# The delta-rule layer of a hybrid decoder on one core: query products behind the joins, the two decay exponentials apart

## The reference, cut to what matters

```python
decay = jnp.exp(jnp.where(causal, gc[..., :, None] - gc[..., None, :], -jnp.inf))
kb = k * beta[..., None]
a = jnp.where(strict, jnp.einsum('bhnid,bhnjd->bhnij', kb, k) * decay, 0.0)
sol = lax.linalg.triangular_solve(a + eye, rhs, left_side=True, lower=True)
u, w = sol[..., :dv], sol[..., dv:]
qk = jnp.where(causal, jnp.einsum('bhnid,bhnjd->bhnij', q, k) * decay, 0.0)
q_dec = q * jnp.exp(gc)[..., None]
def step(state, inp):
    v_new = u_c - jnp.einsum('bhcd,bhde->bhce', w_c, state)
    o = jnp.einsum('bhcd,bhde->bhce', qd_c, state) + jnp.einsum('bhij,bhje->bhie', qk_c, v_new)
    state = state * cd_c[..., None, None] + jnp.einsum('bhcd,bhce->bhde', kd_c, v_new)
    return state, o
```

## Time and profile before

| | |
|---|---|
| median of 3 runs | 3050.88 us (3050.23 to 3052.8) |
| profiled execution, its time | 3050.12 us |
| its span, first to last instruction | 3048.4 us |
| TensorE busy | 2762.6 us (91%) |
| VectorE, ScalarE, GpSimd busy | 1563.2, 866.6, 779.0 us |
| mean granted TensorE clock | 0.95 of full speed |
| delta-rule layer | about 40 to 820 us of the span |
| one head of its loop | 91.7 us |

### The profile page before, as it was taken

One profiled execution on the slowest core, in us unless ns is written; L12 is line 12 of the kernel. 1 busy time (PEld: TensorE's weight loads), 2 busy tenths in 40 slices (PEclk: granted clock), 3 DMA queues, 4 the chain that ended last, 5 costly groups with the idle time before them and its releaser, 6 DMA issues. The chain is left out here.

```text
span 3048.4 us, 35919 instructions
## 1 busy us (share of the span) xinstructions
PE 2762.6 (91%) x13277; PEld 2296.6 (75%) x13277; DVE 1563.2 (51%) x1780; ACT 866.6 (28%) x1213; POOL 779.0 (26%) x372
## 2 busy tenths in 40 slices
PE   7789898888597999999998599999688999999996
PEld 5677777777576888888887487788576888888885
DVE  4455545555234454544455675567354454444555
ACT  5244444344332111111111334333332111111112
POOL 2333223332142222222222211111232222222223
PEclk8799999999798999999999799999898999999998
DMA  2010110010242111111111310110332111111112
GB/s 106 21 42 28 34 41 34 28 41 7 71 151 83 49 48 48 48 41 55 48 48 48 119 35 31 46 48 34 130 119 77 49 41 48 55 48 48 48 62 97
DMA packets 62892, 172.11 MB, mean 56 GB/s; under 512 B 6177, under 2 KB 23137, under 8 KB 62833
## 3 DMA queue, kind: packets, MB, share of 16 engines
q1 hardware_dynamic: 62832, 171.33, 16.5%
HBM read 146.11 MB, written 25.20 MB: 56 GB/s over the span
## 5 line engine op out<-in xcount | busy, mean ns | idle before, releaser
L151 POOL TENSOR_TENSOR f_wlo<-f_raw,f_whi 128x1024 fp32r<-128x1024 f32 x132 | 335.6, 2551 | 1082.8 <-ACT f_whi L171 1082.8
L61 PE MATMUL f_up<-x_hi,f_whi 128*128 128x512 f32 x1408 | 550.4, 391 | 23.0 <-POOL f_wlo L151 23.0
L62 PE MATMUL f_up<-x_lo,f_whi 128*128 128x512 f32 x1408 | 549.7, 390 | 0.0
L63 PE MATMUL f_up<-x_hi,f_wlo 128*128 128x512 f32 x1408 | 549.6, 390 | 0.0
L171 ACT ACTIVATE f_whi<-f_raw 128x1024 fp32r<-128x1024 f32 x132 | 139.8, 1059 | 935.5 <-PE f_up L63 505.9
L61 PEld LDWEIGHTS f_up<-x_hi,f_whi 128*128 128x128 f32 x1408 | 265.6, 189 | 79.1 <-POOL f_wlo L151 23.8
L62 PEld LDWEIGHTS f_up<-x_lo,f_whi 128*128 128x128 f32 x1408 | 265.7, 189 | 55.3
L63 PEld LDWEIGHTS f_up<-x_hi,f_wlo 128*128 128x128 f32 x1408 | 265.4, 189 | 55.5
L61 PE MATMUL f_down<-f_whi,f_hhi 128*128 128x512 f32 x704 | 277.2, 394 | 17.5 <-issue 16.0
L211 DVE TENSOR_TENSOR acc<-f_down,acc 128x512 f32<-128x512 f32 x320 | 217.1, 689 | 123.2 <-PE f_down L63 120.3
L62 PE MATMUL f_down<-f_wlo,f_hhi 128*128 128x512 f32 x704 | 276.3, 392 | 0.0
(11 more groups left out here) (356 smaller groups left out, 4809.6 us busy)
## 6 DMA issues: line engine op xcount, KB each, us to landing
f_raw<-in_ffn_w_up SPq DMA_DIRECT2D x88, 512.0 KB, 3.2
f_raw<-in_ffn_w_down SPq DMA_DIRECT2D x44, 512.0 KB, 3.2
g_raw<-in_gdn_w_in SPq DMA_DIRECT2D x32, 512.0 KB, 3.5
l_raw<-in_gla_w_in SPq DMA_DIRECT2D x26, 512.0 KB, 3.3
after_ffn_xt<-x_mid SPq DMA_DIRECT2D x16, 512.0 KB, 4.1
first_xt<-in_x SPq DMA_DIRECT2D x8, 512.0 KB, 8.1
g_columns<-cum_rows SPq DMA_DIRECT2D x8, 512.0 KB, 3.8
mixed<-g_zc SPq DMA_DIRECT2D x8, 512.0 KB, 2.9
```

Source lines behind the costliest of these rows:

```text
L61: pe.matmul(out, w_hi, x_hi, start=first, stop=False)
L62: pe.matmul(out, w_hi, x_lo, start=False, stop=False)
L63: return pe.matmul(out, w_lo, x_hi, start=False, stop=last)
L151: pool.tensor_tensor(w_lo[k][:, :], raw[k][:, :], w_hi[k][:, :].bitcast(F32), ALU.subtract) \
```

## The change

- **Queries.** TensorE's turn of the queries (`queries_by_token`), ScalarE's squares of them, VectorE's sums of the squares and ScalarE's root move from the end of the scan and the start of `prepare` to behind the last join. The products of queries and keys now wait for the squares. VectorE's reciprocal (`query_factors`) moves to the start of the next `prepare`. One fill that stood between the keys' turn and the keys' products goes to the queries' turn. SiLU of the queries leaves the scan and follows the output norm, and `qdT` (queries times decay from the start) follows the value's convolution.
- **Decay.** The exponential of the columns as loaded (`from_start`) now comes first; then VectorE subtracts in place in `columns`, clamps, and the second exponential goes from `columns` to `decay`. Subtraction and clamp stand before the attention's multiplication, where they stood behind it.
- **ScalarE.** In the loop the eviction of z's second half moves from the end of `prepare` to behind the first `g_vn` copy, `g_vn` comes ahead of it; the output copy and the first join copies come ahead of the value eviction and `high(h, 3)`.
- **GpSimd and VectorE in the scan.** `near_back` comes ahead of the first convolution tap. GpSimd masks (`coupling(h, 0)`) as soon as the lanes are done, ahead of the spreads; in head 0 it also splits the third weight tile before that.

```diff
...
+                if peeled(h):
+                    split(h, 2)
+                pool.wait_ge(s_inverted, h + 1)
+                coupling(h, 0)
...
-                coupling(h, 0)
-                split(h, 2)
+                if not peeled(h):
+                    split(h, 2)
...
-            def decay_exps(h):
-                act.wait_ge(s_dm, h + 1)
-                act.activation(decay[:, :, :], decay[:, :, :], ACT.Exp).then_inc(s_dx, 1)
+            def from_start_exp(h):
...
-                act.activation(from_start[:, :, :], by_chunk(columns), ACT.Exp).then_inc(s_dx, 1)
+                act.activation(from_start[:, :, :], by_chunk(columns), ACT.Exp).then_inc(s_fsx, 1)
+            def decay_exp(h):
+                if not peeled(h):
+                    act.wait_ge(s_ap, h)
+                act.wait_ge(s_dm, h + 1)
+                act.activation(decay[:, :, :], by_chunk(columns), ACT.Exp).then_inc(s_dx, 1)
...
-                              5: lambda: evict(h, 1, 0),
-                              6: lambda: silu(qT, 3 * h + 2)}
+                              5: lambda: evict(h, 1, 0)}
...
+                    if n == 0 and projects and not peeled(h):
+                        evict(h - 1, 3, 1)
...
-                if projects:
-                    act.wait_ge(s_qtok, h + 1)
-                    act.activation(wTn[:, :, :], by_chunk(pm), ACT.Square).then_inc(s_qsq, 1)
-                    evict(h, 1, 1)
-                    if not final(h):
-                        high(h, 3)
+            def query_squares(h):
+                act.wait_ge(s_qtok, h + 1)
+                act.activation(wTn[:, :, :], by_chunk(pm), ACT.Square).then_inc(s_qsq, 1)
+            def query_deviation(h):
+                act.wait_ge(s_qss, h + 1)
+                act.activation(stdq[:, :], ssq[:, :], ACT.Sqrt, bias=eps[:, 0:1]).then_inc(s_qstd, 1)
...
-                m1_copies(h, 0)
+                if peeled(h):
+                    evict(h, 1, 1)
+                    m1_copies(h, 0)
+                else:
+                    m1_copies(h, 0)
+                    evict(h, 1, 1)
+                if not final(h):
+                    high(h, 3)
...
-                act.wait_ge(s_qss, h + 1)
-                act.activation(stdq[:, :], ssq[:, :], ACT.Sqrt, bias=eps[:, 0:1]).then_inc(s_qstd, 1)
-                if not peeled(h):
...
+                silu(qT, 3 * h + 2)
...
+                query_squares(h)
+                if not final(h):
+                    from_start_exp(h + 1)
...
+                    decay_exp(h + 1)
...
-                    decay_exps(h + 1)
...
-                    evict(h, 3, 1)
+                query_deviation(h)
...
-                dve.wait_ge(s_col, 16 * h + 16)
-                dve.tensor_tensor(decay[:, :, :], by_chunk(columns), wide(hg[:, G_CUM, :]), ALU.subtract)
+                dve.wait_ge(s_fsx, h + 1)
+                dve.tensor_tensor(by_chunk(columns), by_chunk(columns), wide(hg[:, G_CUM, :]), ALU.subtract)
...
-                    dve.tensor_reduce(out=x[:, n:B, 0:n], in_=product, axis=AX_X, op=ALU.add, negate=True)
+                    dve.tensor_reduce(out=x[:, n:B, 0:n], in_=product, axis=AX_X, op=ALU.add, negate=True) \
+                        .then_inc(s_inverted, 1)
...
-                              4: lambda: (near_joined(h, True), conv_q(h, (1,))),
-                              5: lambda: near_back(h),
+                              4: lambda: (near_joined(h, True), near_back(h)),
+                              5: lambda: conv_q(h, (1,)),
...
-                        beside[4] = lambda: near_joined(h, True)
-                        del beside[6]
+                        del beside[5], beside[6]
...
+                    query_factors(h - 1)
...
-                dve.tensor_tensor(qdT[:, :, :], by_chunk(qT), from_start[:, :, :], ALU.mult).then_inc(s_qd, 1)
...
-                dve.wait_ge(s_qstd, h + 1)
-                dve.reciprocal(rq[:, :], stdq[:, :])
-                dve.drain()
-                dve.tensor_scalar(rq[:, :], rq[:, :], float(P) ** -0.5, None, ALU.mult)
+                dve.wait_ge(s_silu, 3 * h + 2)
+                dve.tensor_tensor(qdT[:, :, :], by_chunk(qT), from_start[:, :, :], ALU.mult).then_inc(s_qd, 1)
...
+                query_sums(h)
+                if not final(h):
+                    start_head(h + 1)
+                    head_decay(h + 1)
...
-                pe.wait_ge(s_at, h + 1)
...
+                pe.wait_ge(s_qsq, h + 1)
...
-                pe.wait_ge(s_qsq, h + 1)
+                pe.wait_ge(s_at, h + 1)
...
-                query_key_products(h)
+                queries_by_token(h)
...
+                query_key_products(h)
+                fill(h, 26)
...
-                fill(h, 26, 27)
+                fill(h, 27, 28)
...
-                fill(h, 28)
+                fill(h, 29)
...
-                    fill(h, 29, 30)
+                    fill(h, 30)
...
-                    if c == NT - 1:
-                        queries_by_token(h)
```

More of the change, by code:

```diff
@@ L1222, in _ @@
             silu(kT, 1)
-            decay_exps(0)
+            from_start_exp(0)
+            decay_exp(0)
             key_squares(0)
@@ L1527, in body @@
                 prepare(h)
-            heads(dve, body, lambda h: (scan(h, False, True), output_sums(h - 1), output_norm(h - 1),
+            heads(dve, body, lambda h: (scan(h, False, True), query_factors(h - 1), output_sums(h - 1), output_norm(h - 1),
                                         output_gate(h - 1)))
```

31 lines of the change are left out of this document (19 added, 12 removed).

## The result

The changed kernel takes 3059.84 us (median of 11 runs, 3052.93 to 3062.99); the kernel before, in runs beside it, 3050.64 us (11 runs, 3048.83 to 3052.8). The ratio is 1.0027, with a 95% interval of 1.0019 to 1.0035: slower by 9 us, where 15 were predicted. The profiled execution of the changed kernel took 3053.18 us (span 3051.5), at the low end of its runs, so its trace shows only 3 of the 9 us. Where most of the other 6 are is taken up under *Another profile*.

What follows compares the result with a forecast made beforehand. TensorE's queue plus its waits set the length. Six loop heads at +3.7 us (+22), head 0 at -7.5 and head 7 at 0 gave +15 on 3050.12, so 3065 us; range 3036 to 3080.

Steps and rivals of the forecast that it cites:

- Scan: TensorE's scan in a loop head: 38.8 - 7.3 + 5.2 + 0.2 = 36.9 us, with a 3.5 wait at the sixth update.
- The third update: In the scan, the third state update comes behind VectorE's `near_turned`: 0.2 us a head.
- To the first join: From the scan's end to the first join: the 0.71 wait goes, the step becomes 3.1; 0.9 us gained a head.
- Output norm: Before TensorE's turn of the outputs: GpSimd shuts out the second tiny product; wait 3.67 becomes 5.6, 1.95 us lost.
- Query part: From the last join to the next scan: the queries' turn and new waits add 4.6 us a head; 17.63 becomes 22.3.
- The clock: In the scan: one slow stretch goes behind the 3.18 wait, one comes behind the sixth update's, 1.7 us each.
- Rival C: Each 2.4 us wait for the attention brings a slow stretch, 1.7 each in six heads: 3075 us; chance 0.18.
- Head 0: First head: the 12.8 us weight-tile wait and 2 of slow clock go, other waits come: -7.5 (bounds -12 and -4).
- Head 7 and the end: Last head: gains in scan, norm and table load against losses at queries and last scan's first value copy (+1.6): 0.
- Rival A: In the scan, GpSimd's mask does not hold up `near_back`: 3038 us, 3026 with the tiny product free; chance 0.17.
- B: At the output norm, only the output sums escape being shut out: -12, 3053 us, no change; chance 0.10.
- D: The loop is as before and only the first head counts: -7.5, 3043 us; chance 0.10.

Runs made afterwards that it cites:

- Another profile: The changed kernel itself, unedited, profiled once more: 3058.06 us.
- mask_behind_spreads: The changed kernel with GpSimd's first mask put back behind the two spreads: 3040.7 us, ratio 0.9965 to the kernel before.
- second_mask_first: The changed kernel with GpSimd's second mask ahead of the third weight block's split in heads 1 to 7: 3045.7 us, ratio 0.9981 to the kernel before.
- queries_in_scan: The changed kernel with the queries' SiLU, turn and squares put back in the scan: 3069.9 us, ratio 1.0060 to the kernel before.

## Why the prediction was right, and where it was off

The direction and the mechanism of the waits were right, by the steps that it named; the sum was 15 where 9 came, and the term that was wrong is the clock's. Per head of the loop, from the waits in heads 1 to 6:

- *Scan.* The value copies (5.05 to 0.33) and the state (0 to 3.4). Predicted was the wait at the sixth update with 3.5; it is 3.12, by the cause named, which `mask_behind_spreads` shows: the lanes' end releases a mask that shuts out `near_back`'s scalings. The third update, 0.2 predicted, is 0.28.
- *To the first join.* 0.6 of wait gone, 0.9 predicted with the shorter step.
- *Output norm.* 5.57, predicted 5.6, against 3.65 before. The second product of 8 elements was shut out by 2.28, and `second_mask_first` gives 14 us back when it is not. ScalarE's copy ahead of the squares, 1.06, is worth 0.97 of wait and nothing in time that can be told.
- *Query part.* Attention 2.18 (2.4), w's copy 0.8 on average (1.4), keys' copy 0.72 (0.9): 3.85 was predicted as new, 3.25 came. `queries_in_scan` shows that the way back is worse all the same, by 10 us.
- *The clock.* Here the step failed. I took one slow stretch off (behind the 3.18) and put one back (behind the state), 1.7 each, because the new wait is as long as the old one. In the trace the lower clock stood behind the old wait in all six heads and behind the new one in two, with the same 3.1 of wait in all; busy time fell by 6.15. Why the clock fell in two heads and not in four, the runs do not show. Rival C, more slow clock, went the wrong way: the attention's wait has the lower clock behind it in the same two heads, and the total is less. Idle rose by 19.4, where my terms (-1.06 - 0.9 + 1.95 + 3.85 = 3.84 a head) make 23; with the clock the loop is +13.2 and not +22.
- *Head 0.* -7.5 was predicted; -10.9 came in one profile and -6.1 in the other; the early split alone, in the kernel before, gives -14. The two profiles of one kernel differ by 4.85, more than my error in the first. (My terms there, 12.8 + 2 + 0.8, make 15.6 and not 15.4, which changes nothing.)
- *Head 7 and the end.* 0 predicted, -3.5 + 4.4 = +0.9 measured; the 1.6 in front of the last scan's first copy is there.

Rival A is refuted by the trace itself (scalings 3.56, not 1.41), B by the 2.28, D by the loop itself, 13.2 us longer. That the profiled execution took 3053.18, B's very number, is chance: the sums did not escape, and head 0 was in its fast order.

## What to carry to other kernels

- When work is put earlier, look at what its predecessor's end releases on the other engine: here one semaphore started a GpSimd mask exactly when VectorE needed the port. Two instructions of GpSimd changed places for 14 us, one went behind two others for 19 (13 each in the loop of the profiles).
- Split a difference into idle and busy time of the bounding engine. Of single waits removed here the clock took back between nothing (`second_mask_first`) and over half (5.2 of 9.9, 6.6 of 9.2); with two and three of them gone it gave time in addition, and the loop ran at 0.99 and at full clock. The gain of a single edit, measured alone, is then no measure of what it is worth beside others.
- No wait in a profile is not the same as room: take the distance between an operand's end and its use before anything is put ahead of it.
- A gain of 5 us read off one profile each can be a race in a part that was not edited. Look for other kernels with that part unchanged.

## What the runs showed of the hardware

- The exclusion reaches the smallest copies: 8 elements a row from SBUF to SBUF took 1.83 on average, up to 2.34, beside GpSimd, and 0.16 alone. It holds GpSimd up too: its multiplications take 1.9 or 2.4 alone, and 2.9 or 3.4 where they alternate with VectorE's taps.
- A slower TensorE can make the kernel faster: in head 0 a join whose products ran at the lower clock throughout (3.66 us) released a mask just after VectorE had taken up `qdT`, and the first scan started 4.2 to 4.85 us earlier than in three profiles where the products took 2.05, 3.08 and 3.27. Four profiles agree with this; no experiment forced it.
- A wait of one length has the lower clock behind it in some heads and not in others: 0.68 and 1.00 behind 3.12 and 3.11 us.

The Trainium skill ("SBUF — State Buffer", Who interferes with whom) says of the first point that the side that starts first has the pair for its whole instruction and the other blocks fully. The traces agree for single instructions (2.28 us for 8 elements, ended with the mask); that a run of them on both engines then alternates, so that both are slow, is what the earlier trace rows and the two profiles of head 0 add.
